# Issuing the squares of the first-half RMSNorm ahead of the second-half projection

## The reference

```
xn = rms_norm(h, norm_mix_g);  q, k, v, gates = xn @ w_in          # then attention and a short convolution
h = h + mixed @ w_mix_out                                          # projection 1
h = h + cross_attention(rms_norm(h, norm_x_g), memn, ...)          # ends in w_xo: projection 2
f = relu(rms_norm(h, norm_ffn_g) @ w_ff1) ** 2;  h = h + f @ w_ff2 # projection 3
```

## Time and profile before

| | us |
|---|---|
| median of 4 timed runs | 4727.63 (4608.76, 4612.82, 4842.44, 5238.4) |
| the profiled execution's own time | 4597.15 |
| its span, slowest core (core 4) | 4595.3 |
| spans of the eight cores | 4560.3 to 4595.3 |
| TensorE busy in that span | 4267.1 (93%) |
| ScalarE busy | 1675.0 (36%) |
| VectorE busy | 2150.1 (47%) |

### The profile page before, as it was taken

One profiled execution on the slowest core, in us unless ns is written; L12 is line 12 of the kernel. 1 busy time (PEld: TensorE's weight loads), 2 busy tenths in 40 slices (PEclk: granted clock), 3 DMA queues, 4 the chain that ended last, 5 costly groups with the idle time before them and its releaser, 6 DMA issues.

```text
span 4595.3 us, 69827 instructions; the slowest of 8 cores (4560.3 to 4595.3 us)
## 1 busy us (share of the span) xinstructions
PE 4267.1 (93%) x24288; PEld 2073.1 (45%) x24288; DVE 2150.1 (47%) x3450; ACT 1675.0 (36%) x2673; POOL 322.7 (7%) x612
## 2 busy tenths in 40 slices
PE   6988989999998898999979889999999988989998
PEld 2544434444455443444425454344444544434443
DVE  6655335434554425444555443444445544254445
ACT  3266342112336544111333663421123365441112
POOL 0000100000000010000100001000010000100000
PEclk9999999999998999999979889999999989999999
DMA  4200432223220142222442004222232101422224
GB/s 111 45 8 4 66 48 40 40 37 51 40 42 1 24 69 37 40 40 42 90 130 46 1 10 66 44 42 37 40 49 51 26 1 24 69 37 40 39 38 115
DMA packets 108480, 204.36 MB, mean 44 GB/s; under 512 B 12144, under 2 KB 12272, under 8 KB 107632
## 3 DMA queue, kind: packets, MB, share of 16 engines
q0 software_dynamic: 87552, 159.42, 22.7%
q1 hardware_dynamic: 20592, 40.49, 2.9%
HBM read 342.47 MB, written 16.78 MB: 78 GB/s over the span
## 4 chain that ended last, share of the span: by engine, by line
PE 82%; ACT 9%; DVE 4%; issue 4%; SPq 1%; DMA 1%; ACTq 0%; DVEq 0%
PE pp L127 82%; ACT E L127 4%; ACT tF L127 2%; ACT bA L127 1%; DVE tF L127 1%; SPq L127 1%; DVE Ost L127 1%; DVE U L127 1%; DMA hT<-xT 1%; ACT ssb L127 0%; DVE bX L127 0%; DVE hT L127 0%; ACTq L125 0%; DVE obw L127 0%; DVE sqt L127 0%
## 5 line engine op out<-in xcount | busy, mean ns | idle before, releaser
L127 PE MATMUL pp<-bX,wb 128*128 128x512 bf16 x9216 | 2062.3, 382 | 15.8 <-ACT U L127 11.9
L127 PEld LDWEIGHTS pp<-bX,wb 128*128 128x128 bf16 x9216 | 904.0, 98 | 1110.1 <-issue 48.1
L127 PE MATMUL pp<-bA,wb 128*128 128x512 bf16 x4096 | 887.9, 379 | 6.3 <-DVE hT L127 6.2
L127 ACT ACTIVATE E<-pp 128x1024 bf16<-128x1024 f32 (+3 forms) x896 | 700.9, 807 | 412.6 <-PE pp L127 406.7
L127 DVE TENSOR_TENSOR hT<-pp,hT 128x512 f32<-128x512 f32 x768 | 523.3, 690 | 665.8 <-PE pp L127 665.7
L127 ACT ACTIVATE tF<-pp 128x512 f32<-128x512 f32 x576 | 343.9, 597 | 1256.4 <-PE pp L127 1233.3
L127 PEld LDWEIGHTS pp<-bA,wb 128*128 128x128 bf16 x4096 | 400.2, 98 | 490.2 <-issue 8.4
L127 POOL DMA_DIRECT2D wb<-wst x608 | 322.5, 531 | 4241.8 <-PE pp L127 4183.7
L127 DVE TENSOR_TENSOR bA<-tF 128x512 bf16<-128x512 f32 x512 | 353.4, 692 | 522.4 <-ACT tF L127 522.4
L127 PE MATMUL pp<-bA 64*128 64x512 bf16 (+3 forms) x1280 | 331.5, 380 | 118.0 <-ACT E L127 115.7
L127 ACT ACTIVATE bA<-hT 128x512 bf16<-128x512 f32 x448 | 251.3, 618 | 445.7 <-DVE hT L127 277.2
(11 more groups left out here) (77 smaller groups left out, 1994.8 us busy)
## 6 DMA issues: line engine op xcount, KB each, us to landing
wb<-wst POOLq DMA_DIRECT2D x608, 256.0 KB, 3.6
hT<-xT SPq DMA_DIRECT2D x64, 256.0 KB, 12.6
outT<-hT SPq DMA_DIRECT2D x64, 256.0 KB, 2.8
U<-memT SPq DMA_DIRECT2D x4, 1024.0 KB, 6.5
tI<-pos SPq DMA_DIRECT2D x8, 256.0 KB, 3.3
U<-lamg SPq DMA_DIRECT2D x1, 384.0 KB, 6.0
U<-consts SPq DMA_DIRECT2D x1, 192.0 KB, 7.8
cst<-consts SPq DMA_DIRECT2D x1, 48.0 KB, 2.0
```

Source lines behind the costliest of these rows:

```text
L127: ins = getattr(eo, op["name"])(*op["args"], **op["kw"])
```

## The change: what it does

`rms_norm` and `final_norm_range` get an argument `part`. With "sq" they issue the squares of all their tiles and nothing else; with "rest" everything but the squares; with "all" what they did. `resid_gemm` calls "sq" for the first half ahead of step 2, "rest" where the whole norm of the first half stood (step 3), and "all" for the second half (step 5).

```diff
-        def rms_norm(..., src_wide=None, t_lo=0):
+        def rms_norm(..., src_wide=None, t_lo=0, part="all"):
+            if part == "sq":
+                for t0 in range(t_lo, ncols, cn):
+                    for k in range(KC):
+                        S.add("act", lambda e: e.activation(out=bA[:, k, t0:t0 + cn], in_=src_of_k(k, t0, cn), func=AF.Square),
+                              reads=src_keys_of_k(k, t0, cn), writes=tk("bA", k, t0, t0 + cn))
+                return
             for t0 in range(t_lo, ncols, cn):
...
                 for k in range(KC):
-                    if src_wide is None:
+                    if src_wide is None and part == "all":
                         S.add("act", ... func=AF.Square)
                     S.add("pe", ... lhsT=onesD[:], rhs=bA[:, k, t0:t0 + cn] ...)
...
             gemm(6, act_of, act_keys, H, resid_evac, ci0=2)
+            norm_fn(0, H, "sq")
             gemm(2, act_of, act_keys, SEQ, resid_evac, t_lo=H)
-            norm_fn(0, H)
+            norm_fn(0, H, "rest")
             gemm(6, act_of, act_keys, SEQ, resid_evac, t_lo=H, ci0=2)
-            norm_fn(H, SEQ)
+            norm_fn(H, SEQ, "all")
```

More of the change, by code:

```diff
@@ L325, in gemm, with rms_norm @@
                     evac(ci, t0, bank)
-        def rms_norm(src_of_k, src_keys_of_k, gcol, dst_of_k, dst_keys_of_k, ncols, cn, src_wide=None, t_lo=0):
+        def rms_norm(src_of_k, src_keys_of_k, gcol, dst_of_k, dst_keys_of_k, ncols, cn, src_wide=None, t_lo=0, part="all"):
+            if part == "sq":
[4 more added lines that the diff above has]
+                return
             for t0 in range(t_lo, ncols, cn):
@@ L398, in resid_gemm, with final_norm_range @@
             gemm(6, act_of, act_keys, H, resid_evac, ci0=2)
+            norm_fn(0, H, "sq")
             gemm(2, act_of, act_keys, SEQ, resid_evac, t_lo=H)
-            norm_fn(0, H)
+            norm_fn(0, H, "rest")
             gemm(6, act_of, act_keys, SEQ, resid_evac, t_lo=H, ci0=2)
-            norm_fn(H, SEQ)
+            norm_fn(H, SEQ, "all")
             return True
-        def final_norm_range(s, t_lo, t_hi):
+        def final_norm_range(s, t_lo, t_hi, part="all"):
+            if part == "sq":
+                for t0 in range(t_lo, t_hi, TC):
+                    for k in range(KC):
+                        S.add("act", lambda e: e.activation(out=bA[:, k, t0:t0 + TC], in_=hT[:, k, t0:t0 + TC], func=AF.Square),
+                              reads=tk("h", k, t0, t0 + TC), writes=tk("bA", k, t0, t0 + TC))
+                return
             for t0 in range(t_lo, t_hi, TC):
@@ L408, in final_norm_range @@
                 for k in range(KC):
-                    S.add("act", lambda e: e.activation(out=bA[:, k, t0:t0 + TC], in_=hT[:, k, t0:t0 + TC], func=AF.Square),
-                          reads=tk("h", k, t0, t0 + TC), writes=tk("bA", k, t0, t0 + TC))
+                    if part == "all":
+                        S.add("act", lambda e: e.activation(out=bA[:, k, t0:t0 + TC], in_=hT[:, k, t0:t0 + TC], func=AF.Square),
+                              reads=tk("h", k, t0, t0 + TC), writes=tk("bA", k, t0, t0 + TC))
                     S.add("pe", lambda e: e.matmul(ps[bank][:, 0:TC], lhsT=onesD[:], rhs=bA[:, k, t0:t0 + TC],
@@ L649, in build_program @@
                 mix_keys = lambda k, t0, cn: (tk("bX", k, t0, t0 + cn) if k < 4 else tk("bC", k - 4, t0, t0 + cn))
-                n5 = resid_gemm(mix_of, mix_keys, (lambda lo, hi: rms_norm(h_of, h_keys, C_GX + 8 * l, bX_of, bX_keys, hi, TC, t_lo=lo)) if twopass else None,
+                n5 = resid_gemm(mix_of, mix_keys, (lambda lo, hi, part: rms_norm(h_of, h_keys, C_GX + 8 * l, bX_of, bX_keys, hi, TC, t_lo=lo, part=part)) if twopass else None,
                                 inject=lambda: [fn(*a_) for fn, a_ in late_pe]) \
@@ L729, in build_program @@
                               reads=[("tF", f)], writes=[PS(4 + dvc)] + tk("bX", 2 * hh + dvc, t0, t0 + TC))
-                n7 = resid_gemm(bX_of, bX_keys, (lambda lo, hi: rms_norm(h_of, h_keys, C_GFFN + 8 * l, bX_of, bX_keys, hi, TC, t_lo=lo))) \
+                n7 = resid_gemm(bX_of, bX_keys, (lambda lo, hi, part: rms_norm(h_of, h_keys, C_GFFN + 8 * l, bX_of, bX_keys, hi, TC, t_lo=lo, part=part))) \
                     if twopass else (gemm(8, bX_of, bX_keys, SEQ, resid_evac) or False)
@@ L749, in build_program @@
                         if l + 1 < depth:
-                            nfn = lambda lo, hi: rms_norm(h_of, h_keys, C_GMIX + 8 * (l + 1), bX_of, bX_keys, hi, TC, t_lo=lo)
+                            nfn = lambda lo, hi, part: rms_norm(h_of, h_keys, C_GMIX + 8 * (l + 1), bX_of, bX_keys, hi, TC, t_lo=lo, part=part)
                             p1_done = resid_gemm(bA_of, bA_keys, nfn)
                         elif final_norm:
-                            fin_done = resid_gemm(bA_of, bA_keys, lambda lo, hi: final_norm_range(s, lo, hi))
+                            fin_done = resid_gemm(bA_of, bA_keys, lambda lo, hi, part: final_norm_range(s, lo, hi, part))
                         else:
-                            resid_gemm(bA_of, bA_keys, lambda lo, hi: None)
+                            resid_gemm(bA_of, bA_keys, lambda lo, hi, part: None)
                     else:
```

## The result

The changed kernel took 4557.62 us in its profiled execution, which is also the median of its first seven runs. It was compared with the kernel before three times.

| comparison | ratio | 95% interval |
|---|---|---|
| first | 0.9874 | 0.9858 to 0.989 |
| again | 0.9907 | 0.989 to 0.9924 |
| third | 0.9918 | 0.9897 to 0.994 |

The account below looks back on a forecast made before the run. PE, busy 4267 of 4595 us, was taken to bound the kernel, so only its gaps and slow matmuls count. Twelve places gain 46.5 us: 4608.8 - 46.5 = 4562 us (profiled 4597.15 to 4550.7), range 4535 to 4613.

Parts of the forecast that it names:

- The rule: At each of 12 places, tile 0's first normed block to the second half's norm takes 21.77 us; sum gained 46.5 us.
- 3.5 us in hand at the MLP's squares: MLP's projection, the tightest place: squares end 3.4 us before tile 0's logarithm is due, so ACT's part costs nothing.
- 12 new bank waits: PE waits about 1.1 us a place for group 1's bank, one of 2.4, 14 us in all.
- PE's wait for squares: PE's wait for ACT `bA` falls by 28 us plus 1.3 at the table load, to about 70.
- at every such norm: Said in favour of a clock loss after the bank wait: in the kernel before, the clock falls at every such norm.
- The sum: All 12 places together gain 46.5 us: profiled execution 4597.15 to 4550.7 us, fastest timed run 4608.8 to 4562 us.
- Rival A: First-half projections: PE need not wait for group 1's evacuation; gain 61 us, 4548 us; chance 0.08.
- Rivals B and C: After the bank wait the clock falls, 1.7 us a place (B, 4582, 0.09), or stays down long (C, about 4658, 0.03).
- Rival D: Eight extra squares on ACT delay tile 0's logarithm by 4.25 us; -0.4 us a place, 4613 us; chance 0.04.
- Rival E: No effect: the gap reappears elsewhere whole, 4609 us; chance 0.04.
- A measurement of this kernel can tell about 2% from no change, so this counts as the same: Verdict on the forecast 1.0% faster: within 2% given 0.93, over 2% faster 0.04, over 2% slower 0.03.
- Steps after the norm move as a block: Everything behind each norm shifts earlier unchanged, so the sum of 46.5 us reaches the end.

Follow-up runs that it names:

- the two experiments that take it away: Changed kernel with eight PSUM banks instead of six (ratio 0.9871), or with tile 1's norm behind the first of six chunks (fastest run 4537.95 us, no ratio).
- without the two chunks of cover: Changed kernel with the two second-half chunks between squares and onesD matmuls moved behind the norm; no ratio, two fastest runs 4594.87 and 4597.27 us.
- eight banks: Changed kernel with eight PSUM banks instead of six for the six chunks on the second half; ratio 0.9871 to the kernel before.
- norm of tile 1 later: Changed kernel, six banks, with tile 1's norm put behind the first of the six chunks; no ratio, fastest run 4537.95 us.

## Why the prediction was right and where it failed

*The places: right to 1%.* The rule (21.77 us from the first normed block to tile 2's matmuls) measured 21.79 to 21.80. It forecast 46.5 us for core 4, and the places gave 46.2 there and 45.0 on the mean of the cores. Each part of it shows: PE's row of 16 matmuls, 3.62 us long; DVE's row of 16 blocks, 10.69 us (10.7 forecast); 3.5 us in hand at the MLP's squares (3.4); 12 new bank waits of 13.1 us in all (14), the longest 2.3 (2.4); PE's wait for squares down by 27 us on the pair of slowest cores (29); the clock 1.00 where it had been 0.66. One reading was too wide: the clock did not fall "at every such norm". On core 4 it stayed at 1.00 at the fifth place, with the same wait of 2.3 us and the same slow matmuls (window in the last section), and in the two profiles of the kernel before it fell at 173 of 192 places. The sum doesn't use it.

*Where the call stands* has no effect of its own: with the squares called behind the two chunks instead, right ahead of the rest of the norm, the queues and waits of all engines are the same in the two programs, instruction by instruction; no run was made of that order. What the change does is the order on ACT alone.

*Rival A* (no bank wait, 61 us) is refuted by the wait in the trace and by the two experiments that take it away and gain 13 to 14 us more, some 58 and 59 us in all. *Rivals B and C*: the clock is 1.00 through every bank wait, the one of 2.29 us included. The Trainium skill, "TensorE: Matmul & The Clock Gate", section "A second HAM failure mode: psum-queue depth-cycling", tells of a kernel that cycles through PSUM banks and whose PE idles briefly so often between its groups that the clock swings between two levels. The traces show none of it here: a lone bank wait of 0.96 us among dense matmuls cost no clock. *Rival D* is what happens without the two chunks of cover. *Rival E* is refuted by the twelve places.

*The failed step: "A measurement of this kernel can tell about 2% from no change, so this counts as the same".* The time of 4557.6 us is close to the 4562 forecast, but the forecast put 0.93 on a change that could not be told from none, and it was clear in three comparisons out of three, with intervals of 0.2% to either side. The two shorter runs at hand (4608.76 and 4612.82) already agreed within 0.1%, and a forecast of 1% should have been called faster. The mechanism did not fail here; what failed was the view of what the measurement resolves.

*The size that was off*: the first ratio is 1.26%, 58 us, where 46.5 were forecast; the mean of three is 1.0%. The difference is on the side of the kernel before, whose runs there were on the mean 11 and 16 us longer than in the second and third comparison, in no place of the code that I could name. That 4557.6 comes so close to 4562 is in part luck: the same sum from the fastest run of the third comparison, 4591.48, gives 4545. And the sum for the profiled execution was 4550.7, which took 4557.62: it went by one core, and between the slowest cores of the two profiles the places gained 46 us, but the spans only 38.8.

*The other failed step: "Steps after the norm move as a block".* Work does, to 0.8 us in the rest. The clock does not: the stretch with the second layer's attention took 6.7 us longer after the change, and the attention as a whole 2.1 us longer, which is where 45 us of places became 43 of span. The sum put this at nothing. It was paid for being shifted, not for what the change does, as the shifts by 0.9 to 2.6 us show.

## What to carry to other kernels

On an engine that takes its queue in order, look for work whose inputs are long ready but which is queued behind an operation that waits for another engine; moving it ahead is worth the gap and the slow pace behind it, but only if something covers the moved work. Then ask what becomes the next wait when the gap closes: here the evacuation of a bank, queued behind 16 blocks on VectorE, took back almost a quarter of the gain. Two more banks gave it back, and the next wait, for a weight load, showed at one place. And compare stage by stage over all cores before a difference of 10 us in a span of 4500 is put down to an edit.

## What the runs showed of the hardware that was not expected

- The length of one attention stretch changed with a shift of less than a microsecond: 437.5, 427.8, 424.6 and 428.1 us with 0, 0.86, 1.73 and 2.59 us of matmuls added ahead, the granted clock of the whole stretch 0.91 without and 0.96 with 8 matmuls, and most cores of one profile agree to 0.1 us.
- A single bank wait of about 1 us between dense matmuls left the clock at 1.00 at all twelve places on all 16 cores of two profiles, and so did the one of 2.29 us at the table load. A gap of 2.28 us followed by matmuls at 0.52 us each had brought it to 0.66 over 5 us.
- The same gap does not always cost the clock. At the fifth place of the kernel before, core 4, PE waits 2.3 us, the slow matmuls follow, and the clock stays at 1.00:

```profile
1803.00:1808.00 5.00, 4.14 (x16) 1.47 (x16) 4.21 (x8) 4.29 (x9) 0.00 (x0) 1.00 0.00 0
```

- Waits of PE for a weight load of 2.57, 3.35 and 3.54 us (eight banks) were followed by a clock of 0.66 over 5 us, and one of 3.87 us (norm of tile 1 later) by 1.00. So the length of a gap alone does not tell in these traces whether the clock falls.
